# Strassen on all four K quarters of an MLP's first product, with the second product woven in and its residual seeded by ScalarE

## The reference, cut to what matters

```python
def sqrelu_mlp(h, w_in, w_out):          # w_in (2048, 8192), w_out (8192, 2048)
    u = jax.nn.relu(h @ w_in)
    return (u * u) @ w_out
# in the trunk, for each of two layers
h = h + sqrelu_mlp(rms_norm(h, mlp_norm[l]), w_mlp_in[l], w_mlp_out[l])
```

## Time and profile before

| | |
|---|---|
| three runs | 1808.98, 1809.41, 1809.51 us; median 1809.41 |
| profiled execution | span 1807.2 us from its first to its last instruction; its own time is not among what is shown beside its span, so the median of the runs stands for it, 2.2 us above the span |
| granted TensorE clock | 0.999 of full speed (mean) |
| busy | PE 1798.6 us, DVE 1436.0 us, ACT 992.4 us |
| chain that ended last | PE 99% |
| steady pairs (two layers) | 84.73 us from one `turn_u` to the next |

### The profile page before, as it was taken

One profiled execution on the slowest core, in us unless ns is written; L12 is line 12 of the kernel. 1 busy time (PEld: TensorE's weight loads), 2 busy tenths in 40 slices (PEclk: granted clock), 3 DMA queues, 4 the chain that ended last, 5 costly groups with the idle time before them and its releaser, 6 DMA issues.

```text
span 1807.2 us, 23220 instructions
## 1 busy us (share of the span) xinstructions
PE 1798.6 (100%) x8200; PEld 1492.9 (83%) x8200; DVE 1436.0 (79%) x1481; ACT 992.4 (55%) x1099; POOL 13.0 (1%) x17
## 2 busy tenths in 40 slices
PE   9999999999999999999999999999999999999998
PEld 7888888888888888888888888888888888888887
DVE  7898978888887976755557776898888879797966
ACT  7665656464655554643445545664646555565643
POOL 0000000000000000000000000000000000000000
PEclk9999999999999999999999999999999999999999
DMA  8465655564746475566564446465647464645671
GB/s 316 157 209 184 230 187 209 186 221 156 254 159 233 140 256 159 181 193 188 186 192 151 132 161 225 148 209 187 219 157 256 159 233 139 232 169 204 213 253 70
DMA packets 178643, 348.55 MB, mean 193 GB/s; under 512 B 10624, under 2 KB 10752, under 8 KB 178176
## 3 DMA queue, kind: packets, MB, share of 16 engines
q1 hardware_dynamic: 177984, 346.02, 56.7%
q10 hardware_dynamic: 576, 1.44, 0.2%
HBM read 345.32 MB, written 2.10 MB: 192 GB/s over the span
## 4 chain that ended last, share of the span: by engine, by line
PE 99%; issue 0%; DVE 0%; ACT 0%; DVEq 0%; POOLq 0%; POOL 0%
PE bank L1492 25%; PE bank L1494 25%; PE bank L1493 25%; PE bank L1457 6%; PE bank L1459 6%; PE bank L1458 6%; PE bank L1518 1%; PE bank L1484 1%; PE bank L1721 1%; PE bank L1809 0%; PE bank L1736 0%; PE bank L1808 0%; PE bank L1738 0%; PE bank L1856 0%; PE bank L1854 0%
## 5 line engine op out<-in xcount | busy, mean ns | idle before, releaser
L1492 PE MATMUL bank<-w_hi,u_hi_a 128*128 128x512 f32 x896 | 348.7, 389 | 0.0
L1494 PE MATMUL bank<-w_hi,u_lo_a 128*128 128x512 f32 x896 | 348.6, 389 | 0.0
L1493 PE MATMUL bank<-w_lo,u_hi_a 128*128 128x512 f32 x896 | 348.6, 389 | 0.0
L1492 PE MATMUL bank<-w_hi,mix_hi 128*128 128x512 f32 x684 | 267.8, 391 | 0.2
L1494 PE MATMUL bank<-w_hi,mix_lo 128*128 128x512 f32 x684 | 266.2, 389 | 0.0
L1493 PE MATMUL bank<-w_lo,mix_hi 128*128 128x512 f32 x684 | 266.2, 389 | 0.0
L548 ACT ACTIVATE w_hi<-arena 128x2048 fp32r<-128x2048 f32 x100 | 191.6, 1916 | 130.1 <-PE bank L1494 99.9
L910 DVE TENSOR_TENSOR w_lo<-arena,w_hi 128x2048 fp32r<-128x2048 f32 x100 | 227.7, 2287 | 39.8 <-ACT w_hi L548 39.7
L560 ACT ACTIVATE w_hi<-raw 128x1024 fp32r<-128x1024 f32 x112 | 119.1, 1063 | 179.9 <-PE bank L1494 170.0
L541 ACT ACTIVATE w_hi<-raw 128x1024 fp32r<-128x1024 f32 x128 | 133.6, 1062 | 148.4 <-PE bank L1459 142.4
L898 DVE TENSOR_TENSOR w_lo<-raw,w_hi 128x1024 fp32r<-128x1024 f32 x128 | 153.4, 1222 | 72.9 <-ACT w_hi L541 72.3
(11 more groups left out here) (203 smaller groups left out, 2783.0 us busy)
## 6 DMA issues: line engine op xcount, KB each, us to landing
raw<-in_w_mlp_in SPq DMA_DIRECT2D x128, 512.0 KB, 4.7
arena<-in_w_mlp_in SPq DMA_DIRECT2D x128, 512.0 KB, 5.3
raw<-in_w_mlp_out SPq DMA_DIRECT2D x128, 512.0 KB, 6.0
arena<-in_w_mlp_out SPq DMA_DIRECT2D x128, 512.0 KB, 5.1
raw<-in_w_kv SPq DMA_DIRECT2D x64, 512.0 KB, 4.4
raw<-in_w_q SPq DMA_DIRECT2D x32, 512.0 KB, 4.6
raw<-in_w_o SPq DMA_DIRECT2D x32, 512.0 KB, 4.2
raw<-in_pool_w SPq DMA_DIRECT2D x4, 512.0 KB, 9.7
```

Source lines behind the costliest of these rows:

```text
L1492: nc.tensor.matmul(bank[:], hi, w_hi[:, slot, kk, :], start=begin, stop=False)
L1493: nc.tensor.matmul(bank[:], hi, w_lo[:, slot, kk, :], start=False, stop=False)
L1494: return nc.tensor.matmul(bank[:], lo, w_hi[:, slot, kk, :], start=False, stop=end)
```

## The change

All four K quarters of pairs 1 to 7 go through `mix_unit`; `std_unit` and its tiles are gone. A quarter and a column group of the pair before now alternate on PE: unit 0, group 0, unit 1, group 1, unit 2, group 2, unit 3, group 3, then `turn_u`. All quarters use half 0, all column groups half 1. The banks are dealt anew: a group sums into `B_22` (first 128 tokens) and `B_P6` (second 128), in group 3 `B_22` and `B_P2`. `B_P6` also holds a running Strassen product, so ACT copies it out behind each unit and back behind each group. The residual no longer goes through DVE: ACT copies the columns of h into the bank (`out_seed`), PE adds onto them without a start flag (`onto`), and ACT copies the sum back to h (`out_drain`). Pair 1 has one matmul more, which opens `B_22`. The combination of the banks is one add shorter. The last four tokens-by-column groups behind the pairs (`end_add`) stay with DVE.

```diff
+        UNIT_AT, OUT_AT = (0, 11, 22, 33), (7, 18, 29, 40)
+        O_BANKS = ((B_22, B_P6), (B_22, B_P6), (B_22, B_P6), (B_22, B_P2))
+        U_BANKS, U_FIRST = (B_P5, B_P6, B_P7, B_P4), (B_P6, B_P7, B_P4, B_22)
```

SyncE's loads, in `in_pair`:

```diff
-                in_unit(layer, p, 1, 0, at - 6, at - 4)
-                in_unit(layer, p, 0, 1, at - 2, at)
-                in_unit(layer, p, 2, 0, at + 7, at + 8)
-                in_unit(layer, p, 3, 1, at + 10, at + 12)
+                for k in range(4):
+                    in_unit(layer, p, k, 0, at + 11 * k - 5, at + 11 * k - 4)
+                    out_group(layer, p - 1, k, at + 11 * k - 2, at + 11 * k)
```

ScalarE, two helpers and the order in `in_pair`:

```diff
+            def out_seed(layer, p, g, tb):
+                nc.scalar.activation(O_BANKS[g][tb][:], h[:, tb, g * SW:(g + 1) * SW], ACT.Copy).then_inc(out_seeded, 1)
+            def out_drain(layer, p, g, tb):
+                if tb == 0:
+                    act.wait_ge(out_half, p * NG + (OUT_ADDS * layer + g + 1))
+                else:
+                    act.wait_ge(pe_done, o_at(layer, p, g) + 4)
+                nc.scalar.activation(h[:, tb, g * SW:(g + 1) * SW], O_BANKS[g][tb][:], ACT.Copy).then_inc(out_added, 1)
...
+                for k in range(4):
+                    if first and k == 0:
+                        unit(0, range(6))
+                        act.wait_ge(rms_done, 2 * layer + 2)
+                        square_relu(layer, 0, 0)
+                        square_relu(layer, 0, 1)
+                        unit(0, (6,))
+                        out_lot(layer, p - 1, par, 0, 0)
+                        round_u(layer, p - 1, False)
+                        act.wait_ge(bank_opened, layer + 1)
+                        act.wait_ge(h_added, H_MLP[layer])
+                        out_seed(layer, p - 1, 0, 0)
+                    elif k == 0:
+                        unit(0, (0, 1, 2))
+                        for i in (3, 2, 1):
+                            square_relu(layer, p - 1, i)
+                        unit(0, (3, 4))
+                        out_drain(layer, p - 2, 3, 0)
+                        added(layer, p - 1, -1)
+                        out_seed(layer, p - 1, 0, 0)
+                        out_drain(layer, p - 2, 3, 1)
+                        unit(0, (5,))
+                        round_u(layer, p - 1, False)
+                        unit(0, (6,))
+                        out_lot(layer, p - 1, par, 0, 0)
+                    else:
+                        unit(k, (0,))
+                        act.wait_ge(pe_done, at + UNIT_AT[k - 1] + 5)
+                        nc.scalar.activation(p1_copy, B_P6[:], ACT.Copy).then_inc(acc_saved, 1)
+                        act.wait_ge(acc_saved, n + k)
+                        out_seed(layer, p - 1, k - 1, 1)
+                        unit(k, (1, 2, 3, 4, 5))
+                        out_drain(layer, p - 1, k - 1, 0)
+                        added(layer, p - 1, 2 * k - 1)
+                        out_seed(layer, p - 1, k, 0)
+                        unit(k, (6,))
+                        out_drain(layer, p - 1, k - 1, 1)
+                        added(layer, p - 1, 2 * k)
+                        nc.scalar.activation(B_P6[:], p1_copy, ACT.Copy).then_inc(acc_back, 1)
+                        out_lot(layer, p - 1, par, k, 0)
+                    if k == 3:
+                        act.wait_ge(acc_back, n + 3)
+                        copy_p1(layer, p)
+                        out_lot(layer, p - 1, par, k, 1)
+                        square_relu(layer, p, 0)
+                        out_seed(layer, p - 1, k, 1)
+                    else:
+                        out_lot(layer, p - 1, par, k, 1)
```

VectorE's order in `in_pair`:

```diff
+                for k in range(4):
+                    if k == 0 and not second:
+                        c_rest(layer, p - 1)
+                    t1_sum(0, i_landed(layer, p, k))
+                    if k == 0 and second:
+                        unit(0, range(6))
+                        square_relu(layer, 0)
+                        square_relu(layer, 1)
+                        unit(0, (6,))
+                        out_lot(layer, p - 1, par, 0, 0)
+                        u_low(layer, p - 1, False)
+                    elif k == 0:
+                        unit(0, range(5))
+                        u_low(layer, p - 1, False, (0, 1))
+                        unit(0, (5,))
+                        u_low(layer, p - 1, False, (2, 3))
+                        unit(0, (6,))
+                    else:
+                        unit(k, range(7))
+                    if k == 3:
+                        c_11(layer, p)
+                    if not (k == 0 and second):
+                        out_lot(layer, p - 1, par, k, 0)
+                    if k == 3 and isinstance(p, int) and p == NP - 1:
+                        c_rest(layer, p)
+                    out_lot(layer, p - 1, par, k, 1)
```

TensorE's order in `in_pair`, and the body of `out_group`:

```diff
+                for k in range(4):
+                    mix_unit(layer, p, k, at + UNIT_AT[k], (slot + UNIT_AT[k]) % HALVES)
+                    if k == 0:
+                        pe.wait_ge(u_taken, (p + 8 * layer) * 4)
+                    out_group(layer, p - 1, k, (slot + OUT_AT[k]) % HALVES)
+                if not (isinstance(p, int) and p == NP - 1):
+                    turn_u(layer, p)
...
+                for lot in range(2):
+                    if lot == 1 and g == NG - 1 and isinstance(p, int) and p == NP - 2:
+                        turn_u(layer, NP - 1)
+                    for tb in range(TB):
+                        tok = slice(tb * P, (tb + 1) * P)
+                        if tb == 0:
+                            pe.wait_ge(lo_ready, at + (2 * lot + 2))
+                        if lot == 0:
+                            pe.wait_ge(out_seeded, p * (NG * TB) + (OUT_ADDS * TB * layer + TB * g + tb + 1))
+                        for i in (2 * lot, 2 * lot + 1):
+                            for kk in range(2):
+                                hi, lo = tile(2 * i + kk)
+                                last = onto(O_BANKS[g][tb], hi[:, tok], lo[:, tok], (slot + i) % HALVES, kk)
+                            if tb == 1:
+                                last.then_inc(pe_done, 1)
+                            elif i == 3:
+                                last.then_inc(out_half, 1)
```

More of the change, by code:

```diff
@@ L652, in square_relu @@
                 first = isinstance(p, int) and p == 0
-                done = (p + 8 * layer) * 4 + (i + 1 + 2 * (first and i == 1))
+                done = (p + 8 * layer) * 4 + ((1, 4) if first else (1, 4, 3, 2))[i]
                 buf = (hid_11, hid_21, hid_12, hid_22)[i]
@@ new lines, in in_pair, with unit @@
+                first = isinstance(p, int) and p == 1
+                n = p * 3 + (21 * layer - 3)
+                def unit(k, steps):
+                    mix_hi_lots(at + UNIT_AT[k], (slot + UNIT_AT[k]) % HALVES, 0, i_landed(layer, p, k), sums + 4 * k, steps)
+                for k in range(4):
[46 more added lines that the diff above has]
+                        out_lot(layer, p - 1, par, k, 1)
@@ L1568, in mix_unit, with piece @@
[L1568 to L1576 removed]
+            def mix_unit(layer, p, u, at, slot):
+                steady = not isinstance(p, int) or p > 1
+                begin, end = u == 0, u == 3
+                done, drained = (p + 8 * layer) * 4, p * (NG * TB) + (OUT_ADDS * TB * layer - NG * TB)
+                def piece(step, bank, which):
+                    pe.wait_ge(lo_ready, at + step + 1)
+                    mixed(bank, which, u, (slot + step) % HALVES, begin, end or bank is B_P6, u >= 1 and bank is B_P6).then_inc(pe_done, 1)
+                piece(0, B_P1, MIX_11)
@@ L1586, in mix_unit @@
-                pe.wait_ge(lo_ready, at + 5)
-                mixed(B_P5, MIX_S1, u, (slot + 4) % HALVES, begin, end).then_inc(pe_done, 1)
+                elif begin:
+                    pe.wait_ge(out_added, drained)
+                piece(1, B_P2, MIX_12)
+                if begin and not steady:
+                    pe.wait_ge(relu_dve, 2 * layer + 1)
+                piece(2, B_P3, MIX_S4)
+                if begin and steady:
+                    pe.wait_ge(u_taken, done - 3)
+                piece(3, B_P5, MIX_S1)
@@ L1590, in mix_unit @@
                 if begin:
-                    pe.wait_ge(u_taken, done - 3)
-                pe.wait_ge(lo_ready, at + 6)
-                mixed(B_P6, MIX_S2, u, (slot + 5) % HALVES, begin, end).then_inc(pe_done, 1)
+                    pe.wait_ge(u_taken, done - (2 if steady else 3))
+                else:
+                    pe.wait_ge(acc_back, p * 3 + (21 * layer - 3 + u))
+                piece(4, B_P6, MIX_S2)
                 if begin:
-                    pe.wait_ge(u_taken, done - 2)
@@ L1603, in in_pair @@
+                if begin and not steady:
+                    nc.tensor.matmul(B_22[:], mix_hi[:, MIX_22, 0, :], w_hi[:, (slot + 5) % HALVES, 0, :], start=True, stop=True).then_inc(bank_opened, 1)
+                piece(6, B_P4, MIX_22)
             def in_pair(layer, p, par):
```

(3 more changed lines are left out.)

393 lines of the change are left out of this document (138 added, 255 removed).

## The result

The changed kernel takes 1797.28 us (median of 5 runs, 1796.73 to 1798.08) where the kernel before takes 1808.98 beside it: a ratio of 0.9935, 95% interval 0.9924 to 0.9945, or 11.7 us less. Forecast were 1793.6, in a range of 1790.0 to 1804.0. So the time lies in the range, 3.7 us above the forecast.

What follows compares the result with a forecast made beforehand. PE (TensorE) alone was taken to set the time. 1809.4 - 19.0 (matmuls removed) + 0.45 (bank-opening matmuls) + 1.2 (steady pairs) + 1.6 (pair 1) = 1793.6 us, range 1790.0 to 1804.0.

Steps and rivals of the forecast that it cites:

- 84 x 0.2265 = 19.0: On PE, 84 matmuls fewer over both layers, each worth its 0.2265 us slot: 19.0 us saved.
- Pair 1, 0.8 us twice: In pair 1 of each layer, PE waits some 0.8 us for ScalarE's second seed of `B_P6`: 1.6 us in all.
- Steady pairs, 12 x 0.1 = 1.2: VectorE's first-quarter chain has 0.2 us slack before group 0; 0.1 us a pair taken as lost, 1.2 us.
- Seeds at 0.54, ScalarE 63 us, VectorE 75.4: A seed takes ScalarE 0.54 us; per pair of 83.3 us ScalarE needs some 63 and VectorE 75.4, so both fit.
- Costs nothing: the loads keep their number and size.: The DMA loads, unchanged in number and size, add no time: 0 us.
- The step-by-step layout, as if each instruction followed on the last: A steady pair laid out from measured prices: VectorE's first pieces of group 0 ready at 31.2, needed at 31.4.
- rival A: VectorE takes over in the first quarter, its chain 0.3 to 1.4 us late: 1802.0 us at 0.8; chance 0.24.
- the prediction's own sign: The prediction is wrong if a steady pair takes over 84.3 us, or ScalarE's write to PSUM over 0.9 us.
- B: Unit 1's first weights land late, delaying `B_P6`'s second seed by 2.1 us in 12 pairs: 1818 us; chance 0.09.
- C: Seeded banks break PE's density, each of 8 added waits a pair costing 0.11 us: 1806 us; chance 0.04.

Runs made afterwards that it cites:

- experiment 9: The kernel before, with only six of the plain quarter's 48 matmuls left out in each of the 14 pairs: 1792.13 us.
- experiment 6: Changed kernel with experiment 4's loops, Experiment 2's load order, and in pair 1 ScalarE's second pieces, save and second seed taken earlier: 1791.3 us.
- Experiment 2: Changed kernel, with SyncE loading the final norm's row after the first strip of the last four groups, not before it: 1796.64 us.
- experiment 4: Changed kernel, with the loop over pairs 2 to 5 written out without a jump back on all four engines: 1794.88 us.
- experiment 5: Changed kernel, with only VectorE's two-pair loop written out: 1795.36 us; with only the other three engines' written out: 1796.75 us.
- experiment 7: The kernel of experiment 4 plus one unused VectorE reduction in the first quarter of each steady pair: 1807.25 us.
- experiment 3: Changed kernel, with ScalarE in pair 1 saving and seeding the running bank ahead of the first column group's second pieces: 1800.61 us.
- experiment 8: The kernel of experiment 4 with the residual of pairs 0 to 6 back on VectorE, additions at three places: 1860.84, 1864.55 and 1822.8 us.

## Why the prediction was right, and where it fell short

The mechanism was right: PE sets the end, 84 slots go, and the other engines nearly keep up. The sum was 3.5 us too low on the span (1807.2 - 19.0 + 0.45 + 1.2 + 1.6 = 1791.45 against 1794.9). By its steps:

- **84 x 0.2265 = 19.0.** Right: experiment 9's steady pairs fall by 1.36 us each, and the changed kernel has the 8118 matmuls. By the 0.216 us that were worked out from the Trainium skill ("VectorE: DVE Perf Modes", "The TRN2 errata") six would be 1.30; the trace's spacing holds.
- **Pair 1, 0.8 us twice.** Right: the pair fell by 0.33 and 0.35 where 1.36 - 0.23 = 1.13 would go without a wait, so 0.80 and 0.78 were lost, to the seed that was named; in experiment 6, where the seed is in time, the whole 1.13 goes.
- **Steady pairs, 12 x 0.1 = 1.2.** Somewhat dear. Pair 2 of either layer lost 0.26 and 0.27, which experiment 6 gives back with pair 1's wait; the others lost up to 0.05 but for the one behind the jump: 0.7 in all. The chain itself was nearly as worked out. In the pair from 256.66 VectorE passes on from the first pieces of group 0 at 267.65, and group 0's first matmul starts at 267.96, 0.3 us later, where the forecast had 31.64 - 31.2 = 0.4. Less one weight load that is a slack of 0.1; it was put at 0.2.
- **Seeds at 0.54, ScalarE 63 us, VectorE 75.4.** Right: the third window has 62.82 and 75.46. ScalarE's groups by line (busy us, mean ns) give the forms that no row showed:

```profile
L676 ACT ACTIVATE bank<-h 128x512 f32<-128x512 f32 x112 | 67.2, 600 | 8.2 <-PE bank L1614 5.2
L684 ACT ACTIVATE h<-bank 128x512 f32<-128x512 f32 x112 | 65.1, 581 | 2.9 <-PE bank L1516 2.6
...
L657 ACT ACTIVATE arena<-arena 128x512 f32<-128x512 f32 x60 | 38.0, 633 | 2.0
```

  A seed lasts 0.600 us where a square of the same shape from SBUF to SBUF (`L657`) lasts 0.633, and the next instruction starts 0.54 behind it. That the Trainium skill ("ScalarE: Activation LUTs", "Step-by-step: what each stage is for") has ScalarE faster into PSUM than into SBUF agrees with these two rows by 5%, though a copy is compared with a square.
- **"Costs nothing: the loads keep their number and size."** This step failed. Number and size were kept, but not the time at which they are asked for: the end strip's loads stand behind a wait for pair 7's last Strassen unit in SyncE's queue, and the new order put that unit behind three column groups, close to the end. From the `turn_u` of pair 6 (1657.57) to the end the changed kernel takes 137.3 us, as the kernel before did, where 1.36 was to go: 1.4 us lost. Experiment 2 brought 1.3 of it back (136.0).
- **The step-by-step layout, as if each instruction followed on the last.** It left out VectorE's jump back, which costs 2.2 us of PE in one pair of layer 0. Experiments 4 and 5 show it. The kernel before has the same loop, and its steady pairs are all 84.73 long: whatever its jump cost VectorE, slack covered it (experiment 9), and in the new first quarter there is none (experiment 7).

Together 1.4 + 2.2 - 0.5 = 3.1 of the 3.5 us (0.5 is what the steady pairs cost less than their 1.2); the other 0.4 are 0.2 each of the start (first `turn_u` at 93.69 for 93.49) and of pair 7 and the end strips of layer 0.

That the time fell into the range is in part luck: the room above the forecast was made for rival A, and two losses that the sum did not hold took 3.6 us of it. By the prediction's own sign (wrong if a steady pair takes over 84.3 us) the pair from 340.08 fails with 85.60, and PE has gaps outside pair 1.

Of the rivals, A (VectorE late) came true in one pair of 12, and by the jump, not by the prices; experiment 7 shows how near it was, since one more microsecond there left 1.8 us of a gain of 14.3. B did not happen: in the pair from 256.66 the second seed ends at 269.50, 12.8 us behind `turn_u` (33.5 - 20.4 = 13.1 in the forecast), and group 0's second block comes at 270.72. C did not happen: PE is without a gap in pairs with eight such waits.

Not settled: why the jump back stalls VectorE in layer 0 alone. In layer 1 the same instructions run through at 1396.12 without idle. The profile names no releaser, and where the program's code lies was not varied by itself.

## What to carry to other kernels

When work moves off the engine that sets the end, add up the other engines quarter by quarter, in the order of their queues: VectorE had 8 us a pair to spare by its share, and none in the one quarter that counted. Follow every wait in the DMA queue that hangs on a mark of an engine whose order changes, since the loads behind it move with the mark. Before an early instruction is put ahead of another, ask who waits for the one that it delays: experiments 3 and 8 each took a wait away, and the time rose.

## What the runs showed of the hardware that was not expected

A jump back cost VectorE 2.1 to 2.8 us (10.54 to 11.21 us over the same instructions, 8.44 without the jump), at the same place in each of the five profiles in which VectorE jumps, in one layer and not in the other. And of twelve gaps of 2.4 us on PE (experiment 8, first kernel) three were followed, 1.0 to 1.5 us after the restart, by some 3 us at a granted clock of 0.50; behind the other nine, and behind the gap of 1.08 us in front of the changed kernel's end strip, it stayed at 1.00. What parts the three from the nine, the runs do not show.
